# Recurrent outputs into dead input tiles, and a pair's decay sums into the chunks of the pair before

## The chip, the cores and the metric

The kernel runs on one core of one Trainium2 chip. The metric is device time in microseconds, the median of several runs. Engines: PE (matmuls), DVE (elementwise), ACT (activations and copies), POOL (elementwise, its own queue of transfers) and SP, which only issues transfers. Each runs its own list of instructions in order, and they wait for one another on semaphores.

## What is computed

One step of a decoder layer over 512 prompt tokens and 8 x 4 sample tokens (544 columns in all): three gated branches (sparse attention, RWKV-7 time mixing, cross-attention), then a squared-ReLU MLP. The change touches the second branch alone:

```python
def rwkv7_time_mix(p_b, shift_prev, wkv_prev, mu, ...):
    ps = p_b + (prev - p_b) * mu                      # prev: p_b one token earlier
    r, k, v, wl, al, gl = split_last(ps, RWKV_SIZES)
    w_log = -softplus(-(w0 + tanh(wl) @ w_up)) - 0.5
    decay = exp(-exp(w_log)); a = sigmoid(a0 + al @ a_up); g = sigmoid(gl) @ g_up
    kk = heads(k * k_k); kk = kk / max(sqrt(sum(kk * kk)), 1e-12)
    k_h = heads(k) * (1 + (a_h - 1) * k_a)
    # step: S = S*w_t + (S @ -kk_t)(kk_t*a_t)^T + v_t k_t^T ;  y_t = S @ r_t
    yn = (y - mean) * rsqrt(var + GN_EPS) * ln_g + ln_b   # group norm, per head
    bonus = sum(r_h * k_h * r_k) * v_h
    out = (yn + bonus) * g
```

## The kernel before

Everything lies with features on the 128 partitions and the 544 tokens along the columns. `pb3[:, t]` are the 14 projected tiles of the RWKV branch, each 553 columns wide: 0 to 3 hold r, 4 to 7 k, 8 to 11 v, for the four head pairs j (two heads of 64 features make one tile). `R` is a scratch area; its first slots of 544 columns are `r_`, `k__`, `v__`, `lw`, `L_`, `a_`, `kk`, `kh`, then `AR` (two), `bt`, `kt_`, `tA`, `tB`, each used by all four pairs in turn. `y_` is another name for `r_`.

A loop over j = 0 to 3 stands in every engine's list. For one pair the stages are, in PE's order:

- **prep**: DVE mixes r (`mix`, L2140 and L2143, from POOL's token difference `diff`, L814 to L818), sums the log-decays along the tokens (the scan L2228 into `L_`), takes off each chunk's middle (`c0`, L2234), notes the chunks' ends (`scf`, L2235 and L2236) and subtracts (L2237 into `a_`, signalled by `lx`). ACT then makes four exponentials (L1823 to L1826: `tA`, `tB`, `lw`, `scf`). DVE multiplies: L2243 (r, k and r_k into `L_`, signalled by `rk`), the factors `AR`, `bt`, `kt_`. PE sums `L_` over each head with the block matrix `blk` (the call `wide(6, ...)`, inside which the matmul is L1286), DVE makes the bonus of that into `L_` (L2250).
- **tm** and **inv**: PE transposes v, `bt`, `kt_` (L1328), and inverts a small triangular system by stages.
- **chunk** c = 0 to 3: 128 tokens each. PE computes z, u, the state's increment and y; ACT copies them out (y into `y_`); DVE updates the state `T0` (L2297, L2298). Beside it the next pair's work that needs no buffer of this pair is done, by calls of `early(j + 1, n)`: mixing k and v, `kk`, the decays and `a_`, the norm of `kk`.
- **dec**: the same recurrence for the sample tokens, with masks on DVE (from L2314 on) after products on PE (L1486 to L1488). PE first waits for the root of `kk` (ACT's L1789).
- **gn**: the group norm. PE sums `y_` by `blk`, DVE subtracts the mean (L2344), ACT squares and takes the root (L1910), DVE does `early(j + 1, 5)` and `(j + 1, 6)` (L2183; L2186 and L2187, which make `kh`), one or two weight conversions, the reciprocal (L2354) into `tB`, the product (L2355), `ln_g` and `ln_b` (L2359), the bonus (L2360) and the gate g (L2362), which goes into `pb3[:, j]` and signals `oB_out`.

Between these stages PE's list holds **fill** steps: pieces of other projections (the gates of the three branches), placed by `fill_plan` in fixed numbers per place (8 at each of three places in prep, 10 behind the transposes' wait, 2, 2 and 4 in a chunk, 4 in each part of dec, 6, 6 and 10 in gn). From the gates on a step is three matmuls (L980, L981, L982) on weights split in two parts: ACT copies the high part (`weights_hi`, L554), DVE makes the low part (`weights_lo`, L564, which I call a conversion). ACT evacuates a finished half of a gate by a tanh (L1653). In ACT's list the evacuations (`evacs`) stand at the places of the fills.

What sets the order at a turn from one pair to the next: POOL's `diff(r_, j)` waits for `oB_out`, since `r_` is `y_`; DVE's mix waits for that; the scan writes `L_`, which held the bonus until L2360.

## Time and profile before

| | |
|---|---|
| median of 3 runs | 1305.33 us (1304.65 to 1307.05) |
| the profiled execution: time, span | 1306.21 us, 1304.4 us |
| PE busy | 1218.8 us, 93% of the span |
| DVE, ACT, POOL busy | 707.3 us (54%), 407.4 us (31%), 88.1 us (7%) |
| mean granted clock of PE | 0.982 of full speed |
| transfers | 127.64 MB, 98 GB/s over the span |

A PE that is busy for 93% hides much of what the others do. The four pairs take the stretch from some 350 to 770 us. Timelines give the start and the length of each instruction and, in brackets, how long its engine was idle before it and what ended that. Lengths overlap a little: an engine's next instruction starts before the one before it is over. On PE three matmuls of a fill step start 0.126 us apart at full clock. The granted clock of a stretch is a share of full speed: 1.00 is 2.4 GHz, 0.50 is 1.2 GHz, and a value between means that it changed within the stretch.

### The profile page before, as it was taken

The page shows a single profiled execution, that of the slowest core. Times are in us where ns is not written, and L with a number is a line of the kernel's source. Part 1 is how long each engine was busy: PE and PEld are TensorE (multiplying, and loading weights), DVE is VectorE, ACT ScalarE, POOL GpSimd, SP SyncE. Part 2 cuts the span into 40 slices and gives each one's busy share as a digit, 9 for nine tenths or more (in the row PEclk, how much of TensorE's full clock was granted, in tenths as well). Part 3 has the DMA queues.
Part 4 walks back from the last instruction along what each step waited for, and adds up shares of the span by engine and source line. Part 5 has one row for each costly group of instructions (what it writes and reads, how often), then busy time and mean ns, then how long its engine had stood idle before and what let it go on. Part 6 is the DMA issues. An engine that isn't in the chain of part 4 may idle for free.

```text
span 1304.4 us, 25158 instructions
## 1 busy us (share of the span) xinstructions
PE 1218.8 (93%) x10594; PEld 1085.5 (83%) x10594; DVE 707.3 (54%) x1126; ACT 407.4 (31%) x792; POOL 88.1 (7%) x148
## 2 busy tenths in 40 slices
PE   7999987899999979989989999999999999999994
PEld 6658765577777778888878889999999999999994
DVE  6799998422431753473383267654535434444445
ACT  2111445334224332343333333233333133132120
POOL 1100000011020520002001020000000000000000
PEclk9999999999999989999999999999999999999997
DMA  9122535043100220131123125641222222222201
GB/s 333 41 102 85 200 118 182 33 162 130 77 11 34 82 91 11 60 107 51 52 93 109 37 86 169 210 169 65 98 86 109 74 88 98 92 71 97 97 33 69
DMA packets 39507, 127.64 MB, mean 98 GB/s; under 512 B 5235, under 2 KB 17523, under 8 KB 30179
## 3 DMA queue, kind: packets, MB, share of 16 engines
q1 hardware_dynamic: 36674, 120.95, 26.4%
q0 software_dynamic: 1440, 4.56, 1.0%
q8 instruction: 84, 1.38, 0.4%
q10 hardware_dynamic: 1280, 0.53, 0.2%
q14 instruction: 29, 0.23, 0.1%
HBM read 111.88 MB, written 14.13 MB: 97 GB/s over the span
## 4 chain that ended last, share of the span: by engine, by line
PE 75%; DVE 14%; SPq 4%; issue 3%; ACT 3%; DMA 1%; POOL 0%; DVEq 0%; ACTq 0%
PE ps L944 13%; PE ps L943 13%; PE ps L947 13%; PE ps L971 7%; PE ps L1335 4%; PE ps L980 4%; PE ps L981 3%; PE ps L982 3%; SPq L582 2%; SPq L581 2%; DVE R L2050 2%; PE ps L1286 2%; DVE small L2049 1%; PE ps L1072 1%; DVE R L2354 1%
## 5 line engine op out<-in xcount | busy, mean ns | idle before, releaser
L554 ACT ACTIVATE wh<-land 128x1024 fp32r<-128x1024 f32 (+1 forms) x120 | 116.2, 970 | 184.8 <-PE ps L947 184.8
L564 DVE TENSOR_TENSOR wl<-land,wh 128x1024 fp32r<-128x1024 f32 (+1 forms) x120 | 134.9, 1127 | 29.9 <-ACT wh L554 29.1
L971 PE MATMUL ps<-xn,ring 128*128 128x272 f32 x576 | 148.4, 400 | 0.0
L943 PE MATMUL ps<-xhi,wh 128*128 128x272 f32 x512 | 138.2, 288 | 2.3 <-DVE wl L564 1.2
L944 PE MATMUL ps<-hl,wh 128*128 128x272 f32 x512 | 138.2, 289 | 0.0
L944 PE MATMUL ps<-xlo,wh 128*128 128x272 f32 x512 | 138.1, 289 | 0.0
L943 PE MATMUL ps<-hh,wh 128*128 128x272 f32 x512 | 138.1, 288 | 0.0
L980 PE MATMUL ps<-xhi,wh 128*128 128x272 f32 x384 | 124.7, 325 | 2.3 <-issue 2.3
L971 PEld LDWEIGHTS ps<-xn,ring 128*128 128x128 f32 x576 | 104.1, 190 | 24.3 <-issue 6.2
L981 PE MATMUL ps<-xlo,wh 128*128 128x272 f32 x384 | 113.5, 295 | 0.0
L982 PE MATMUL ps<-xhi,wl 128*128 128x272 f32 x384 | 113.4, 295 | 0.0
L947 PE MATMUL ps<-hh,wl 128*128 128x272 f32 x512 | 106.1, 288 | 0.0
L947 PE MATMUL ps<-xhi,wl 128*128 128x272 f32 x512 | 106.1, 288 | 0.0
L943 PEld LDWEIGHTS ps<-xhi,wh 128*128 128x128 f32 x512 | 96.3, 188 | 2.9 <-DVE wl L564 1.7
L944 PEld LDWEIGHTS ps<-hl,wh 128*128 128x128 f32 x512 | 96.4, 188 | 0.0
L944 PEld LDWEIGHTS ps<-xlo,wh 128*128 128x128 f32 x512 | 96.4, 188 | 0.0
L943 PEld LDWEIGHTS ps<-hh,wh 128*128 128x128 f32 x512 | 96.3, 188 | 0.0
L980 PEld LDWEIGHTS ps<-xhi,wh 128*128 128x128 f32 x384 | 75.2, 196 | 13.0 <-issue 9.6
L947 PEld LDWEIGHTS ps<-xhi,wl 128*128 128x128 f32 x512 | 80.1, 188 | 0.0
L947 PEld LDWEIGHTS ps<-hh,wl 128*128 128x128 f32 x512 | 80.1, 188 | 0.0
L2398 DVE TENSOR_TENSOR mlpt<-mlpt 128x544 f32<-128x544 f32 x32 | 23.2, 724 | 104.8 <-ACT mlpt L1618 104.8
L2412 DVE TENSOR_TENSOR scaled<-ps,scaled 128x544 f32<-128x544 f32 x32 | 23.2, 725 | 102.4 <-PE ps L947 102.4
(413 smaller groups left out, 2351.3 us busy)
## 6 DMA issues: line engine op xcount, KB each, us to landing
land<-in_slabs SPq DMA_DIRECT2D x48, 1024.0 KB, 4.8
ring<-in_slabs SPq DMA_DIRECT2D x17, 1024.0 KB, 6.9
gates<-R SPq DMA_DIRECT2D x24, 272.0 KB, 2.0
merge<-gates SPq DMA_DIRECT2D x24, 272.0 KB, 4.2
land<-in_slabs SPq DMA_DIRECT2D x12, 512.0 KB, 3.9
xT<-in_mks SPq DMA_DIRECT2D x8, 512.0 KB, 5.7
R<-in_kv SPq DMA_DIRECT2D x24, 128.0 KB, 2.0
pb<-in_kv SPq DMA_DIRECT2D x24, 128.0 KB, 2.0
```

The lines of the kernel that those rows point to most:

```text
L554: act.activation(hi, src, ACT.Copy).then_inc(s["weights_hi"], 1)
L564: eng.tensor_tensor(lo, src, hi.bitcast(F32), ALU.subtract).then_inc(s["weights_lo"], 1)
L581: pg = eng.value_load(pages[0:1, 8 * b + j:8 * b + j + 1], min_val=0, max_val=i["ki"].shape[0] - 1)
L582: eng.dma_start(dst, pages_of[bass.ds(pg, 1)].rearrange("o p c -> (o p) c")).then_inc(sem, 16)
L943: pe.matmul(ps[:, b + h, 0:HALF], whi[:, k], hi[k][:, c], start=a, stop=False)
L944: pe.matmul(ps[:, b + h, 0:HALF], whi[:, k], lo[k][:, c], start=False, stop=False)
L947: mm = pe.matmul(ps[:, b + h, 0:HALF], wlo[:, k], hi[k][:, c], start=False, stop=z)
L971: mm = pe.matmul(ps[:, b, 0:HALF], W[:, k, c0_:c0_ + w], xn3[:, k, cols], start=a, stop=z)
L980: pe.matmul(ps[:, b, 0:HALF], whi[:, k], X[0][k][:, cols], start=a, stop=False)
L981: pe.matmul(ps[:, b, 0:HALF], whi[:, k], X[1][k][:, cols], start=False, stop=False)
L982: mm = pe.matmul(ps[:, b, 0:HALF], wlo[:, k], X[0][k][:, cols], start=False, stop=z)
L1335: mm = pe.matmul(out[q], left[q], right[q], start=True, stop=True)
```

## The change

Two buffers get separate homes for the time in which they collided. y of pair j goes into `pb3[:, j]`, the r input tile, which is dead once r is mixed; the bonus of pairs 0 to 2 into `pb3[:, 4 + j]`, the k input tile (pair 3 keeps `L_`). With that, `r_` and `L_` are free for the next pair while this one runs its chunks:

- POOL's `diff(r_, j + 1)` follows those of k and v, in pair j's inv stage, and no longer waits for `oB_out`.
- DVE does the next pair's scan and centring (`decay_sums`) in the third chunk, and the r mix, the ends and the subtraction (`decay_ends`, now into `lw`) and `early(j + 1, 6)` in the fourth.
- `bt` is made in gn, in the place where `early(j + 1, 6)` stood.
- ACT's exponentials wait for DVE's product y times `tB` (one count of `lx` more per pair) and stand ahead of the evacuations of prep's first place; that place's weight splits go with them.
- Of the two conversions that DVE had ahead of the exponentials' wait, the first stays ahead of it, the second follows the factors.

```diff
-        y_ = r_
+        def y_of(j):
+            return pb3[:, j, 0:TOK]
+        def bonus_of(j):
+            return pb3[:, 4 + j, 0:TOK] if j < 3 else L_
...
@@ POOL, for j in range(4)
-                if j:
-                    pool.wait_ge(s["oB_out"], j)
-                else:
+                if j == 0:
                     pool.wait_ge(s["t12"], 2)
-                diff(r_, j)
+                    diff(r_, 0)
...
                     diff(v__, 9 + j)
+                    diff(r_, j + 1)
...
@@ ACT, for j in range(4)
                     evacs("scan", 0)
-                else:
-                    evacs("prep", j, 0)
-                act.wait_ge(s["lx"], j + 1)
+                act.wait_ge(s["lx"], 2 * j + 1)
                 act.activation(tA, L_, ACT.Exp).then_inc(s["exps"], 1)
                 act.activation(tB, L_, ACT.Exp, scale=-1.0).then_inc(s["exps"], 1)
-                act.activation(lw, a_, ACT.Exp).then_inc(s["exps"], 1)
+                act.activation(lw, lw, ACT.Exp).then_inc(s["exps"], 1)
                 act.activation(scf, scf, ACT.Exp).then_inc(s["exps"], 1)
+                if j:
+                    evacs("prep", j, 0)
                 evacs("prep", j, 1)
...
@@ DVE
+            def decay_sums():
+                step(dve.tensor_tensor_scan(L_, k_("reset"), lw, 0.0, ALU.mult, ALU.add))
+                step(dve.tensor_copy(c0, L_[:, C // 2 - 1:SEQ:C]))
+                l3 = L_[:, 0:SEQ].rearrange("p (c t) -> p c t", c=4)
+                step(dve.tensor_tensor(l3, l3, c0.unsqueeze(2).to_broadcast([P, 4, C]), ALU.subtract))
+            def decay_ends():
+                step(dve.tensor_copy(scf, L_[:, C - 1:SEQ:C]))
+                step(dve.tensor_tensor(scf[:, 0:3], scf[:, 0:3], c0[:, 1:4], ALU.add))
+                dve.tensor_tensor(lw, L_, lw, ALU.subtract).then_inc(s["lx"], 1)
...
+                    mix(r_, 0, 4)
+                    decay_sums()
+                    dve.tensor_tensor(bt, kk, a_, ALU.mult)
+                    decay_ends()
                 else:
-                    dve.wait_ge(s["oB_out"], j)
-                mix(r_, j, 4 + 3 * j)
-                step(dve.tensor_tensor_scan(L_, k_("reset"), lw, 0.0, ALU.mult, ALU.add))
-                dve.tensor_tensor(bt, kk, a_, ALU.mult)
+                    weights_lo(dve, g + 2)
...
-                if j:
-                    weights_lo(dve, g + 2)
-                    weights_lo(dve, g + 3)
                 dve.wait_ge(s["exps"], 4 * (j + 1))
...
                 dve.tensor_tensor(kt_, kh, tB, ALU.mult).then_inc(s["factors"], 1)
+                if j:
+                    weights_lo(dve, g + 3)
                 dve.wait_ge(s["rk_sum"], j + 1)
-                dve.tensor_tensor(h2(L_), pair(6), h2(v__), ALU.mult).then_inc(s["bonus"], 1)
+                dve.tensor_tensor(h2(bonus_of(j)), pair(6), h2(v__), ALU.mult).then_inc(s["bonus"], 1)
...
                             early(j + 1, m)
+                        if c == 2:
+                            decay_sums()
+                        elif c == 3:
+                            mix(r_, j + 1, 4 + 3 * (j + 1))
+                            dve.wait_ge(s["state"], 4 * (j + 1))
+                            decay_ends()
+                            early(j + 1, 6)
...
                     early(j + 1, 5)
-                    early(j + 1, 6)
+                    dve.tensor_tensor(bt, kk, a_, ALU.mult)
...
                 step(dve.reciprocal(tB, tA))
-                step(dve.tensor_tensor(y_, y_, tB, ALU.mult))
+                if j < 3:
+                    dve.tensor_tensor(y_, y_, tB, ALU.mult).then_inc(s["lx"], 1)
+                    dve.wait_ge(s["lx"], 2 * j + 3)
+                else:
+                    step(dve.tensor_tensor(y_, y_, tB, ALU.mult))
...
-                step(dve.tensor_tensor(y_, y_, L_, ALU.add))
+                step(dve.tensor_tensor(y_, y_, bonus_of(j), ALU.add))
```

How instructions stand on an engine, before and after (line numbers differ between the two files). DVE at the end of pair 1's fourth chunk, from the state's update to the first sample mask, before:

```order
L2297 TENSOR_TENSOR small<-small,ps 128x64
L2298 TENSOR_SCALAR small<-small 128x64
L2314 TENSOR_TENSOR xT<-ps,cst 32x128
L2316 TENSOR_TENSOR xT<-ps,cst 32x32
L2318 TENSOR_TENSOR xT<-xT,cst 32x32
```

The same place after:

```order
L2308 TENSOR_TENSOR small<-small,ps 128x64
L2309 TENSOR_SCALAR small<-small 128x64
L2145 SCALAR_TENSOR_TENSOR R<-R,vec,pb 128x512
L2148 SCALAR_TENSOR_TENSOR R<-R,vec,pb 128x32
L2234 COPY small<-R 128x4
L2235 TENSOR_TENSOR small<-small 128x3
L2236 TENSOR_TENSOR R<-R 128x544
L2191 TENSOR_SCALAR R<-R,vec 128x544
L2192 SCALAR_TENSOR_TENSOR R<-R 128x544
L2332 TENSOR_TENSOR xT<-ps,cst 32x128
```

Seven operations, the r mix, the decays' ends and the two that make `kh`, now stand between the state's update and the masks.

DVE from the gate's product in pair 1 to L2243 in pair 2, before (the scan is printed as SCALAR_TENSOR_TENSOR with `cst`):

```order
L2362 TENSOR_TENSOR pb<-ps,R 128x544
L2140 SCALAR_TENSOR_TENSOR R<-R,vec,pb 128x512
L2143 SCALAR_TENSOR_TENSOR R<-R,vec,pb 128x32
L2228 SCALAR_TENSOR_TENSOR R<-cst,R 128x544
L2229 TENSOR_TENSOR R<-R 128x544
L2232 COPY small<-R 128x4
L2234 TENSOR_TENSOR R<-R,small 128x512
L2235 COPY small<-R 128x4
L2236 TENSOR_TENSOR small<-small 128x3
L2237 TENSOR_TENSOR R<-R 128x544
L564 TENSOR_TENSOR wl<-land,wh 128x1024 x2
L2243 SCALAR_TENSOR_TENSOR R<-R,vec 128x544
```

The same stretch after, from the group norm's reciprocal on:

```order
L2373 RECIPROCAL R<-R 128x544
L2375 TENSOR_TENSOR pb<-pb,R 128x544
L2382 TENSOR_SCALAR pb<-pb,vec 128x544
L2383 TENSOR_TENSOR pb<-pb 128x544
L2385 TENSOR_TENSOR pb<-ps,pb 128x544
L570 TENSOR_TENSOR wl<-land,wh 128x1024
L2252 SCALAR_TENSOR_TENSOR R<-R,vec 128x544
```

The nine operations from the mix to the subtraction and one of two conversions are gone from between the gate's product (L2362, now L2385) and L2243 (now L2252).

ACT at the turn from pair 0 to pair 1, from the group norm's root to the exponentials, before:

```order
L1910 ACTIVATE R<-ps,small 128x544
L1646 ACTIVATE pb<-ps 128x240
L1647 ACTIVATE pb<-ps 128x8x4
L1653 ACT_TABLE_LOAD
L1653 ACTIVATE R<-ps,small 128x272 x2
L554 ACTIVATE wh<-land 128x1024 x2
L1823 ACTIVATE R<-R 128x544
```

And after:

```order
L1915 ACTIVATE R<-ps,small 128x544
L1651 ACTIVATE pb<-ps 128x240
L1652 ACTIVATE pb<-ps 128x8x4
L1658 ACT_TABLE_LOAD
L1658 ACTIVATE R<-ps,small 128x272
L1826 ACTIVATE R<-R 128x544
L1827 ACTIVATE R<-R 128x544
L1828 ACTIVATE R<-R 128x544
L1829 ACTIVATE small<-small 128x4
L1658 ACTIVATE R<-ps,small 128x272
L560 ACTIVATE wh<-land 128x1024 x2
```

One gate evacuation and two weight splits have moved from ahead of the exponentials to behind them.

## Rows read from the trace of the kernel before

**Rows 1.** PE's waits: line, waited for, us in total, times, longest.

```profile
PE ps L1286 <- DVE R L2243: 13.0, 3, 5.0
```

**Rows 2.** Timeline of PE, turn from pair 0 to 1: start, length, instruction.

```profile
446.23 0.36 PE L980 MATMUL ps<-xhi,wh 128*128 128x272 f32 x1 [2.26 <-issue]
463.73 2.18 PE L1286 MATMUL ps<-R,cst 128*128 128x272 f32 x4 [5.02 <-DVE R L2243]
474.86 0.33 PE L1328 MATMUL ps<-cst,R 128*128 128x128 f32 x1 [0.58 <-ACT R L1653]
```

**Rows 3.** Timeline of PE, the other two turns.

```profile
574.13 1.18 PE L1286 MATMUL ps<-R,cst 128*128 128x272 f32 x4 [3.98 <-DVE R L2243]
...
584.19 0.33 PE L1328 MATMUL ps<-cst,R 128*128 128x128 f32 x1 [0.58 <-ACT R L1653]
...
681.94 0.82 PE L1286 MATMUL ps<-R,cst 128*128 128x272 f32 x1 [3.98 <-DVE R L2243]
...
693.18 0.33 PE L1328 MATMUL ps<-cst,R 128*128 128x128 f32 x1 [0.58 <-ACT R L1653]
```

**Rows 4.** Windows: length, busy us (count) of PE, PEld, DVE, ACT, POOL, clock, DMA.

```profile
449.11:458.16 9.05, 9.05 (x74) 9.05 (x73) 7.18 (x9) 2.87 (x4) 2.82 (x7) 1.00 0.45 170
463.73:469.10 5.37, 5.37 (x19) 4.91 (x20) 3.52 (x7) 1.43 (x2) 0.00 (x0) 0.50 0.62 229
537.00:541.00 4.00, 3.95 (x31) 3.69 (x32) 1.14 (x7) 1.49 (x2) 0.00 (x0) 0.58 0.02 4
```

**Rows 5.** Timeline of DVE, turn from pair 0 to 1.

```profile
441.04 1.26 DVE L2183 TENSOR_TENSOR R<-R 128x544 f32<-128x544 f32 x1
...
444.46 3.36 DVE L564 TENSOR_TENSOR wl<-land,wh 128x1024 fp32r<-128x1024 f32 x2
...
451.32 0.73 DVE L2355 TENSOR_TENSOR R<-R 128x544 f32<-128x544 f32 x1
...
460.62 2.35 DVE L564 TENSOR_TENSOR wl<-land,wh 128x1024 fp32r<-128x1024 f32 x2
462.89 0.78 DVE L2243 SCALAR_TENSOR_TENSOR R<-R,vec 128x544 f32<-128x544 f32 x1
```

**Rows 6.** Timeline of ACT, the same turn.

```profile
444.49 1.28 ACT L1653 ACT_TABLE_LOAD   x1
...
453.45 0.49 ACT L1653 ACTIVATE R<-ps,small 128x272 f32<-128x272 f32 x1 [2.51 <-PE ps L982]
453.84 2.00 ACT L554 ACTIVATE wh<-land 128x1024 fp32r<-128x1024 f32 x2
460.74 0.66 ACT L1823 ACTIVATE R<-R 128x544 f32<-128x544 f32 x1 [4.91 <-DVE R L2237]
```

**Rows 7.** Timeline of DVE, turn from pair 1 to 2.

```profile
554.96 0.72 DVE L2183 TENSOR_TENSOR R<-R 128x544 f32<-128x544 f32 x1
...
557.01 1.22 DVE L564 TENSOR_TENSOR wl<-land,wh 128x1024 fp32r<-128x1024 f32 x1
...
561.73 0.73 DVE L2355 TENSOR_TENSOR R<-R 128x544 f32<-128x544 f32 x1
...
566.27 0.75 DVE L2140 SCALAR_TENSOR_TENSOR R<-R,vec,pb 128x512 f32<-128x512 f32 x1 [1.69 <-POOL R L818]
...
567.10 1.28 DVE L2228 TENSOR_TENSOR_SCAN R<-cst,R 128x544 f32<-128x544 f32 x1
...
569.99 0.17 DVE L2235 COPY small<-R 128x4 f32<-128x4 f32 x1
...
571.03 2.35 DVE L564 TENSOR_TENSOR wl<-land,wh 128x1024 fp32r<-128x1024 f32 x2
```

**Rows 8.** Timeline of POOL in pair 0's group norm.

```profile
437.18 12.73 POOL L872 TENSOR_TENSOR xlo<-xn,xhi 128x272 fp32r<-128x272 f32 x12 [0.93 <-PE ps L971]
```

**Rows 9.** Timeline of DVE behind pair 1's last chunk.

```profile
537.53 0.28 DVE L2314 TENSOR_TENSOR xT<-ps,cst 32x128 f32<-32x128 f32 x1 [3.44 <-PE ps L1488]
```

**Rows 10.** Timeline of PE at the same place.

```profile
537.05 0.27 PE L1486 MATMUL ps<-R 64*32 64x64 f32 x2 [1.60 <-issue]
```

More of the change, by code:

```diff
@@ L1526, in _ @@
                 pe.wait_ge(s["s_y_out"], 2 * (j + 1))
-                wide(0, k_("blk"), y_).then_inc(s["mean"], 1)
+                wide(0, k_("blk"), y_of(j)).then_inc(s["mean"], 1)
                 fill("gn", j, 0)
@@ L1873, in _ @@
                     act.wait_ge(s["ychunk"], n + 1)
-                    act.activation(y_[:, C * c:C * (c + 1)], ps[:, 6, 0:P], ACT.Copy).then_inc(s["y_chunk"], 1)
+                    act.activation(y_of(j)[:, C * c:C * (c + 1)], ps[:, 6, 0:P], ACT.Copy).then_inc(s["y_chunk"], 1)
                     if j < 3:
@@ L1902, in _ @@
                     act.wait_ge(s["s_y"], n + 1)
-                    act.activation(y_[hp, SEQ:TOK], ps[hp, 4 + hh, 256:256 + NS], ACT.Copy).then_inc(s["s_y_out"], 1)
+                    act.activation(y_of(j)[hp, SEQ:TOK], ps[hp, 4 + hh, 256:256 + NS], ACT.Copy).then_inc(s["s_y_out"], 1)
                 evacs("dec", j, 3)
@@ L1906, in _ @@
                 act.wait_ge(s["yc"], j + 1)
-                act.activation(tA, y_, ACT.Square).then_inc(s["yc_sq"], 1)
+                act.activation(tA, y_of(j), ACT.Square).then_inc(s["yc_sq"], 1)
                 evacs("gn", j, 0)
@@ L2224, in _ @@
                         early(0, n)
-                else:
-                    dve.wait_ge(s["oB_out"], j)
-                mix(r_, j, 4 + 3 * j)
-                step(dve.tensor_tensor_scan(L_, k_("reset"), lw, 0.0, ALU.mult, ALU.add))
-                dve.tensor_tensor(bt, kk, a_, ALU.mult)
+                    mix(r_, 0, 4)
+                    decay_sums()
+                    dve.tensor_tensor(bt, kk, a_, ALU.mult)
+                    decay_ends()
+                else:
+                    weights_lo(dve, g + 2)
                 dve.wait_ge(s["mix"], 2 + 3 * (j + 1))
-                step(dve.tensor_copy(c0, L_[:, C // 2 - 1:SEQ:C]))
-                l3 = L_[:, 0:SEQ].rearrange("p (c t) -> p c t", c=4)
-                step(dve.tensor_tensor(l3, l3, c0.unsqueeze(2).to_broadcast([P, 4, C]), ALU.subtract))
-                step(dve.tensor_copy(scf, L_[:, C - 1:SEQ:C]))
-                step(dve.tensor_tensor(scf[:, 0:3], scf[:, 0:3], c0[:, 1:4], ALU.add))
-                dve.tensor_tensor(a_, L_, lw, ALU.subtract).then_inc(s["lx"], 1)
-                if j:
-                    weights_lo(dve, g + 2)
-                    weights_lo(dve, g + 3)
                 dve.wait_ge(s["exps"], 4 * (j + 1))
@@ L2343, in _ @@
                 dve.wait_ge(s["mean"], j + 1)
+                y_ = y_of(j)
                 dve.scalar_tensor_tensor(h2(y_), pair(0), -1.0 / 64, h2(y_), ALU.mult, ALU.add).then_inc(s["yc"], 1)
```

## The prediction

> **What bounds the kernel now.** I read the page first: PE is busy for 93% of the span (the table above), so time can only go where PE waits or runs slowly. PE's list of waits is the second view. The longest wait in the part that the change touches is L1286, the `blk` product that sums the bonus, on DVE's L2243: 13.0 us in 3 times, the longest 5.0 [rows 1]. There is one at each turn from a head pair to the next. Third, PE's timeline at the turn from pair 0 to pair 1 [rows 2]: PE has used up the fill steps that it may do, comes to the product at 458.71 (463.73 less 5.02) and starts it at 463.73. The other two turns wait 3.98 us each [rows 3]. The clock shows that the wait costs more than its length: in the 5.37 us after it the granted clock is 0.50, the lower of the two levels (1.2 GHz), PE having stood still just before [rows 4].
>
> Then the timelines of DVE and ACT at that turn tell what ends last [rows 5, 6]. DVE finishes the group norm, waits for POOL's token difference, mixes r, scans, centres and only then frees ACT's exponentials (460.74); two weight conversions later comes L2243 at 462.89. At the turn from 1 to 2 the same stretch, mix to the end of the last subtraction, runs from 566.27 to 571.03 [rows 7], behind a group-norm product (L2355) that was over at 562.46. From there to L2243 lies nothing that needs the group norm's result, only its buffers: y and r share one, the bonus and the scan share another. That is what the change undoes.
>
> **Part 1, the wait.** After the change the exponentials need tA and tB free, that is the end of L2355, and nothing else that is late. Turn 0 to 1: L2355 ends at 452.05 now; part 3 brings that to 451.2. The exponentials take at most 2.15 us (460.74 to the reader at 462.89): 453.35. ACT now evacuates a gate half and splits weights behind them (0.49 and, for the first of two, 1.0) [rows 6]: 454.8. DVE, whose last three group-norm operations end by 453.3, waits for that, converts (half of 2.35: 1.18) and does L2243 (0.78): 456.8. PE comes at 458.71 less 0.9, 457.8. Margin 1.0 us, the wait is gone. Turn 1 to 2: 562.46 plus 2.15 for the exponentials and as much for DVE's three operations beside them (they end at 564.58, 566.27 less 1.69 [rows 7]), one conversion, L2243: 566.6, where PE comes at 574.13 less 3.98, 570.15. Margin 3.6 us; turn 2 to 3 repeats it. I take all 13.0 us. What is late next: PE itself. The transposes (L1328) want bonus and factors, and 18 fill steps, 6.8 us, lie between; the conversion put in front of the bonus fits there.
>
> **Part 2, the clock after the wait.** A fill step, three matmuls, takes 0.377 us at full clock: 74 matmuls, two of them cut by the edges, so 24 steps, in 9.05 us [rows 4]. From the product to the transposes there are the product (1.18 at the turn from 1 to 2 [rows 3], the next matmul starting inside it; I take 0.9), 18 steps (6.8), the tail of the last matmul (taken as 0.16) and the wait for its evacuation (0.58): 8.44 us. It took 11.13, 10.06 and 11.24 [rows 2, 3]. Excess 2.7 + 1.6 + 2.8 = 7.1 us. With no standstill ahead of it I count all of it as gained. Bounds: 0, if the clock falls anyway, and 7.1.
>
> **Part 3, a shorter queue before pair 0's first weights.** PE also stands 2.26 us at 446.23 until DVE has converted the first gate weights, a conversion that starts at 444.46 behind two operations for the next pair (L2186, L2187) after 442.30 [rows 2, 5]. The change takes these two (2.16 us) out and puts one product (`bt`) in. L2183 beside POOL's conversions took 1.26 there [rows 5] and 0.72 alone [rows 7], so `bt` costs 0.76 to 1.3 and the gain is 0.9 to 1.4. I take 0.9, since POOL is busy to 449.9 [rows 8]. The Trainium skill, "SBUF — State Buffer", says under its rules on contention that the port pair of DVE and GpSimd is an exclusive lock, so that the loser blocks for the other's whole instruction. By that `bt` could wait for a full POOL piece (12.73 over 12, 1.06 us) and the gain would be 0.4, half a microsecond less in the sum; the 0.54 us that L2183 lost is half such a piece.
>
> **Part 4, what the chunks take on.** About 5.4 us of DVE work per pair move into pairs 0 to 2: into the third chunk the scan, copy and centring (567.10 to 571.03 without `bt` and the last 1.04: about 2.25 us), into the last chunk the mix (0.83), the ends of the decay (1.04) and the two kh operations (1.3, from 557.01 less 554.96, less L2183): 3.2 us [rows 7]. PE needs DVE next when the state is updated and, after the last chunk, for the sample masks (L2314). In pair 1 DVE has nothing to do for 3.44 us ahead of 537.53, when PE's products reach it [rows 9], so 3.2 us just fit; PE itself stands 1.60 us there, until 537.05, for a square root on ACT that does not move [rows 10]. Behind the masks PE still has four fill steps, 1.5 us. I cost it at nothing; without that cover it is at most 3 x 5.4. The weight conversion behind the third chunk comes 2.2 us later, and its weights are wanted a chunk and more later. POOL does one token difference more before the state's DMA, 1.7 us by DVE's wait on one at 566.27, with most of a pair to spare. SP's queue keeps its order. ACT stores y into another tile with the same shape. The odd pitch of the new tiles is free for the reads that show it (L2140 reads such a tile), and where DVE writes there it has the margins above.
>
> **Sum.** 13.0 + 7.1 + 0.9 = 21.0 us. The profiled execution has a span of 1304.4 and a time of 1306.21; 1283.4 and 1285.2 would follow. Against the median of the runs, 1305.33, it is **1284.3**.
>
> **Rivals.** *The turn from 0 to 1 keeps a wait.* Its margin is only 1.0 us and hangs on ACT's evacuation and split in one row. If ACT is 2.6 us later than I count, 1.6 us of wait stay and with them that turn's 2.7 us of slow clock: 1284.3 + 4.3 = 1288.6. For it: conversions beside POOL take longer, 3.36 for two against 2.35 [rows 5]. Against: POOL ends before them.
>
> *A short wait at every turn, and the clock falls all the same.* The 1.60 us standstill in pair 1 is followed by 0.58 of the clock [rows 4, 10], so a short wait can be enough. Three waits of 1.6 and the whole 7.1 kept: 1284.3 + 11.9 = 1296.2. Against: 3.6 us of margin at two turns.
> A path to it: the exponentials now follow the norm's square root on ACT. A table load took 1.28 us at 444.49, ahead of a gate's tanh [rows 6]; one ahead of the exponentials would use up the first margin and leave 2.3 at the others, a wait of 0.3 at one turn. I see none there now, and the tanh still comes between: 1 in 50, inside this rival.
> The Trainium skill, "ScalarE: Activation LUTs", section on table sets, charges 2.66 us for every switch between the sets of root and exponential, which would make that wait 1.7 us; it puts tanh and exp in one set, as the trace does with no load at L1823.
>
> *The chunks pay.* The moved DVE operations run late into the sample masks, all 5.4 us of them on PE's path, and each new standstill costs a slow stretch like the first turn's: 3 x (5.4 + 2.7) = 24.3, less 21.0: **1308.6, slower**. It begins to cost when the last chunk's share exceeds 3.44 us, and turns the sign only if PE's own fill steps cover none of it. Operations 1.75 times as long, as beside POOL, would do the first; POOL is idle in that chunk.
>
> *Nothing moves.* The weights' supply paces the fill steps, so PE waits for conversions instead: about 1305. Against: PE's waits on conversions are at pair 0's start and behind the pairs only.
>
> **How the numbers follow.** Forecast 0.72, first turn late 0.11, short wait at every turn 0.08, nothing moves 0.04, chunks pay 0.05. Within the forecast the slow stretch of pair 1 (12 matmuls at half pace, about 1.3 us) may vanish or another may come, and part 3 has 0.5 either way: 1281.5 to 1287. With the first rival and half the way to the second the range is 1280.5 to 1292, which leaves out under 2 in 10. A measurement of this kernel tells 0.2%, 2.6 us, from no change. Faster by more: 0.91; within: 0.04; slower: 0.05.
>
> **What would show it.** Right: PE has no wait on the `blk` product of the bonus, granted clock 1.00 from there to the transposes, about 8.4 us between them; the exponentials start within 0.2 us of the end of the y product; the first gate's wait is near 1.4 us; the pairs' chunks keep their length. Wrong: a wait of PE for the masks behind the last chunk, an idle ACT before the exponentials that ends with DVE long after the group norm, or the clock at 0.50 in the old places without a wait ahead of it.

## The result, and the profile after

The changed kernel takes **1283.22 us** (median of 6 runs, 1281.55 to 1284.41) against 1304.7 for the kernel before beside it: a ratio of 0.983, 95% interval 0.982 to 0.984, **faster by 21.5 us**. The forecast was 1284.3 with a range of 1280.5 to 1292. Run again later, beside the experiments e7, e8 and e9, it took 1283.61 (1282.02 to 1284.83); that is the base for all of them below. A few executions (three of the kernel before, two each of e1 and e4, one each of e3 and e5) were 1 to 2% longer than the rest at a lower mean granted clock; the medians are over all runs, and leaving these out moves none by more than 0.7 us. The profiled execution took 1281.81 us with a span of 1280.0, 24.4 us less than the profiled one of before.

In the changed file the lines have moved: the `blk` product is L1291 (was L1286), the transposes L1333, the product of r L2252 (was L2243), the group norm's product L2375, the first exponential L1826, a weight conversion L570.

PE's list of waits no longer has the bonus product. PE's timeline at the turn from pair 0 to 1 and at the next turn, which answer to [rows 2, 3] (start, length, instruction, idle before):

```profile
445.12 0.36 PE L985 MATMUL ps<-xhi,wh 128*128 128x272 f32 x1 [1.33 <-ACT pb L1652]
...
457.44 1.08 PE L1291 MATMUL ps<-R,cst 128*128 128x272 f32 x4
...
465.88 0.66 PE L1333 MATMUL ps<-cst,R 128*128 128x128 f32 x4 [0.58 <-ACT R L1658]
...
559.49 1.08 PE L1291 MATMUL ps<-R,cst 128*128 128x272 f32 x4
...
567.94 0.66 PE L1333 MATMUL ps<-cst,R 128*128 128x128 f32 x4 [0.58 <-ACT R L1658]
```

The rows of the two products show no idle time ahead of them, and product to transposes takes 8.44 and 8.45 us (forecast 8.44). The windows between them at the three turns (length, busy time of PE, PEld, DVE, ACT and POOL with counts, granted clock, DMA) answer to the second line of [rows 4]:

```profile
457.44:465.88 8.44, 7.87 (x60) 7.49 (x58) 4.28 (x6) 2.46 (x5) 0.00 (x0) 1.00 0.49 159
559.49:567.94 8.45, 7.88 (x60) 7.50 (x58) 1.95 (x2) 2.46 (x5) 0.00 (x0) 1.00 0.46 157
661.53:669.98 8.45, 7.87 (x61) 7.50 (x59) 1.95 (x2) 2.46 (x5) 0.00 (x0) 1.00 0.46 159
```

The granted clock is 1.00 in all three, where it was 0.50 just behind the first wait. DVE and ACT at the first turn, DVE first, which answer to [rows 5, 6]:

```profile
442.15 1.17 DVE L2366 TENSOR_TENSOR R<-R 128x544 f32<-128x544 f32 x1
443.24 3.48 DVE L570 TENSOR_TENSOR wl<-land,wh 128x1024 fp32r<-128x1024 f32 x2
...
450.22 0.72 DVE L2375 TENSOR_TENSOR pb<-pb,R 128x544 f32<-128x544 f32 x1
...
454.18 1.23 DVE L570 TENSOR_TENSOR wl<-land,wh 128x1024 fp32r<-128x1024 f32 x1 [1.12 <-ACT wh L560]
455.32 0.78 DVE L2252 SCALAR_TENSOR_TENSOR R<-R,vec 128x544 f32<-128x544 f32 x1
...
459.77 0.72 DVE L2261 TENSOR_TENSOR pb<-ps,R 128x544 f32<-128x544 f32 x1
```

```profile
444.31 1.28 ACT L1658 ACT_TABLE_LOAD   x1
...
450.98 0.66 ACT L1826 ACTIVATE R<-R 128x544 f32<-128x544 f32 x1 [1.15 <-DVE pb L2375]
```

The exponentials start 0.04 us after the group norm's product ends (450.94), where they waited 4.91 us for the scan's last subtraction. The product of r ends at 456.1, PE comes at 457.44: a margin of 1.3 us, forecast 1.0. At the next turn L2252 ends at 555.7 and PE comes at 559.49: 3.8, forecast 3.6. No table load stands ahead of L1826; the one for the tanh came at 444.31, as before.

Behind pair 1's last chunk, DVE and then PE, which answer to [rows 9, 10]:

```profile
528.62 0.28 DVE L2332 TENSOR_TENSOR xT<-ps,cst 32x128 f32<-32x128 f32 x1 [0.48 <-PE ps L1493]
```

```profile
528.07 0.27 PE L1491 MATMUL ps<-R 64*32 64x64 f32 x2 [1.60 <-issue]
```

DVE's 3.44 us of idle time ahead of the sample masks have become 0.48: the moved work just fits, as forecast.

**Where the 24.4 us of the two profiled executions went.** 13.0 is the wait. Product to transposes took 11.13, 10.06 and 11.24 and takes 8.44, 8.45 and 8.45: 7.1. The first gate's wait went from 2.26 to 1.33: 0.9. That is 21.0, the forecast's sum. 0.5 more lies in how the waits are counted: the gap starts where the last matmul ends (458.71 at the first turn), 0.16 us after the next could have started (458.55), at each of three turns. The other 2.9 show when the starts of the same PE instruction are set side by side.

1.5 is a stretch of slow clock in pair 1's sample part which the changed kernel's execution does not have, though PE stands 1.60 us ahead of it in both: the changed kernel leads by 8.98 us at the sample products (537.05 against 528.07) and by 10.47 a few products on (541.22 against 530.75). In windows of the kernel before:

```profile
536.00:538.00 2.00, 0.95 (x14) 0.94 (x15) 0.43 (x3) 1.97 (x3) 0.00 (x0) 0.91 0.01 1
538.00:540.00 2.00, 2.00 (x11) 2.00 (x11) 0.60 (x4) 0.14 (x1) 0.00 (x0) 0.50 0.04 8
540.00:542.00 2.00, 2.00 (x39) 1.66 (x40) 0.29 (x2) 0.49 (x1) 0.00 (x0) 0.74 0.00 0
```

Length times one less the clock is 0.18 + 1.0 + 0.52, 1.7 us, an estimate that takes PE as the bound there. A second such stretch of the kernel before alone, behind the pairs, is worth nothing, although its first window looks the same. It follows a wait of 2.33 us for weights that both executions have (at 779.27 and 756.07). The changed kernel, which runs on at full clock, then waits once more for weights, and the kernel before does not. Window and waits of the kernel before, then of the changed one:

```profile
780.00:782.00 2.00, 2.00 (x12) 2.00 (x11) 1.97 (x4) 0.80 (x2) 0.00 (x0) 0.50 0.26 102
PE ps L943 <- DVE wl L564: 3.6, 2, 2.3
```

```profile
PE ps L948 <- DVE wl L570: 5.0, 3, 2.3
...
763.96 0.36 PE L948 MATMUL ps<-bhi,wh 128*128 128x272 f32 x1 [1.42 <-DVE wl L570]
```

The lead is 23.2 us ahead of the stretch and 23.2 again at that instruction (787.15 against 763.96). Of the rest, 1.0 lies in the last stretch of the kernel, from PE's last products to the end (14.77 us from 1289.63, 13.77 from 1266.23): the clock is at 0.50 there in both, but in the changed kernel's execution it fell only after these products. 0.4 lies in small pieces elsewhere. Other executions have such stretches in other places (below), so the medians differ by 21.5 and not by 24.4.

### The profile page after: what moved, and what is told of

Read it like the earlier page. It is cut to its first block, busy times and chain, and to the rows that moved or that the text cites. A ratio compares the mean times of both kernels' runs of the same rounds, so it can differ in the third digit from the quotient of the medians.

```text
span 1280.0 us, 25157 instructions
## 1 busy us (share of the span) xinstructions
PE 1206.3 (94%) x10594; PEld 1075.2 (84%) x10594; DVE 707.1 (55%) x1126; ACT 407.8 (32%) x792; POOL 87.8 (7%) x148
## 3 DMA queue, kind: packets, MB, share of 16 engines
q8 instruction: 84, 1.38, 0.4%
## 4 chain that ended last, share of the span: by engine, by line
PE 80%; DVE 10%; SPq 4%; ACT 3%; issue 3%; DMA 1%; DVEq 0%; ACTq 0%
PE ps L949 13%; PE ps L948 13%; PE ps L952 13%; PE ps L976 8%; PE ps L985 5%; PE ps L1340 4%; PE ps L987 4%; PE ps L986 4%; SPq L588 2%; PE ps L1291 2%; SPq L587 2%; DVE R L2055 2%; DVE small L2054 1%; PE ps L1077 1%; DVE small L2120 1%
## 5 line engine op out<-in xcount | busy, mean ns | idle before, releaser
L570 DVE TENSOR_TENSOR wl<-land,wh 128x1024 fp32r<-128x1024 f32 (+1 forms) x120 | 135.3, 1128 | 26.7 <-ACT wh L560 25.9
L948 PE MATMUL ps<-xhi,wh 128*128 128x272 f32 x512 | 138.2, 288 | 2.3 <-DVE wl L570 1.2
L949 PE MATMUL ps<-xlo,wh 128*128 128x272 f32 x512 | 138.1, 289 | 0.0
L985 PE MATMUL ps<-xhi,wh 128*128 128x272 f32 x384 | 121.3, 316 | 1.3 <-ACT pb L1652 1.3
L987 PE MATMUL ps<-xhi,wl 128*128 128x272 f32 x384 | 110.8, 289 | 0.0
L986 PE MATMUL ps<-xlo,wh 128*128 128x272 f32 x384 | 110.6, 288 | 0.0
L952 PE MATMUL ps<-xhi,wl 128*128 128x272 f32 x512 | 106.1, 288 | 0.0
L948 PEld LDWEIGHTS ps<-xhi,wh 128*128 128x128 f32 x512 | 96.3, 188 | 2.9 <-DVE wl L570 1.7
L985 PEld LDWEIGHTS ps<-xhi,wh 128*128 128x128 f32 x384 | 72.2, 188 | 11.9 <-issue 7.0
L2421 DVE TENSOR_TENSOR mlpt<-mlpt 128x544 f32<-128x544 f32 x32 | 23.2, 724 | 104.8 <-ACT mlpt L1623 104.8
L2435 DVE TENSOR_TENSOR scaled<-ps,scaled 128x544 f32<-128x544 f32 x32 | 23.2, 725 | 102.4 <-PE ps L952 102.4
```

Source lines behind the costliest of these rows:

```text
L570: eng.tensor_tensor(lo, src, hi.bitcast(F32), ALU.subtract).then_inc(s["weights_lo"], 1)
L948: pe.matmul(ps[:, b + h, 0:HALF], whi[:, k], hi[k][:, c], start=a, stop=False)
L949: pe.matmul(ps[:, b + h, 0:HALF], whi[:, k], lo[k][:, c], start=False, stop=False)
L952: mm = pe.matmul(ps[:, b + h, 0:HALF], wlo[:, k], hi[k][:, c], start=False, stop=z)
L985: pe.matmul(ps[:, b, 0:HALF], whi[:, k], X[0][k][:, cols], start=a, stop=False)
L986: pe.matmul(ps[:, b, 0:HALF], whi[:, k], X[1][k][:, cols], start=False, stop=False)
```

## The experiments

All times are medians, set against 1283.6 for the changed kernel and 1306.1 to 1306.6 for the one before, which ran beside each group of them. Lines shift a little in the experiments' files: in the rows below L2254 is the product of r, L2146 the mix of r, L2261 or L2263 the bonus, L2336 or L2337 the last operation of the sample masks, and L1495 or L1497 the product that reads it.

### Is the slow clock the standstill's doing?

**e1_pe_busy**: the kernel before, with PE given something to do while it waits.

```diff
+                for n in range((0, 11, 8, 8)[j]):
+                    pe.matmul(ps[:, n % 2, 0:HALF], k_("blk"), t13[:, 0:HALF], start=True, stop=True)
                 pe.wait_ge(s["rk"], j + 1)
                 wide(6, k_("blk"), L_).then_inc(s["rk_sum"], 1)
```

> The kernel before, with products whose results nobody reads put on PE just ahead of its wait for the bonus product: 11 of 128x272 at the turn from pair 0 to 1 and 8 at each of the other two, about 0.46 us each (two took 0.92 us at full clock), so 5.1 and 3.7 us where PE stood 5.0, 4.0 and 4.0. DVE is as late as before. Theory (the slow stretch follows PE's standstill): the wait ends when it did, but the granted clock stays at 1.00 behind it, product to transposes is about 8.4 us at each turn, and 7 us of the time go: about 1297.6 us. Rival A (the clock falls there anyway, by what the chip does at that time): no gain, 1304 to 1305, the clock at 0.50 in the same places. Rival B (only the first turn's wait is long enough): 2.7 us, 1302.

It took 1299.68 us, 6.6 less than the kernel before. Ten of its twelve runs lie between 1298.9 and 1301.3, below all 28 of the kernel before (1304.6 to 1308.7); over all twelve the 95% interval of the ratio is 0.994 to 1.000. The windows from the product to the transposes:

```profile
466.26:474.70 8.44, 7.86 (x59) 7.49 (x57) 3.07 (x4) 2.46 (x5) 0.00 (x0) 1.00 0.32 131
572.48:581.03 8.55, 7.98 (x58) 7.60 (x58) 4.42 (x7) 2.46 (x5) 0.00 (x0) 1.00 0.45 157
678.79:687.33 8.54, 7.97 (x58) 7.59 (x58) 4.42 (x7) 2.46 (x5) 0.00 (x0) 1.00 0.44 155
```

DVE is as late as before (10.83 us from the end of the group norm's product to the product of r, 10.84 in the kernel before) and the clock holds at 1.00. The theory holds, and rivals A and B fall: part 2's 7.1 us are a cost of PE's standing still, and they can be had even without removing the wait. The time is 2 us above the theory's 1297.6, and 1.5 of that is the edit's own doing: at the first turn the added products ran on past the product of r, which had ended at 464.76.

```profile
461.21 5.21 PE L1316 MATMUL ps<-pb,cst 128*128 128x272 f32 x22
466.26 1.08 PE L1286 MATMUL ps<-R,cst 128*128 128x272 f32 x4
```

**e5_dve_late_7us** and **e4_dve_late_3us** go the other way: the changed kernel with DVE made late again, by two reciprocals or by one (the edit of e5; e4 has a 1 for the 2).

```diff
+                for _ in range(2 if j else 0):
+                    step(dve.reciprocal(L_, tA))
                 dve.scalar_tensor_tensor(L_, r_, v_("rwkv_r_k", j), kh, ALU.mult, ALU.mult).then_inc(s["rk"], 1)
```

> The changed kernel with two reciprocals of 3.54 us, whose results are overwritten, on DVE just ahead of the product that PE's bonus sum waits for, in pairs 1 to 3. Theory: PE waits there again, 5.8 us at the first turn (margin 1.3 less 7.1) and 3.3 at the other two (margin 3.8), 12.4 in all, and the clock falls behind each wait as it did in the kernel before, 2.7 + 1.6 + 2.8 us: 1283.2 + 19.5 = 1302.7. Rival (the clock was not the wait's doing): 1283.2 + 12.4 = 1295.6, granted clock 1.00 behind the waits.

It took 1302.16 us (1298.8 in the profiled execution). PE's waits and the three windows behind them, in that execution:

```profile
PE ps L1291 <- DVE R L2254: 12.3, 3, 5.7
```

```profile
464.21:474.31 10.10, 9.53 (x58) 8.84 (x58) 5.56 (x8) 2.46 (x5) 0.00 (x0) 0.84 0.41 133
571.37:580.42 9.05, 8.20 (x58) 7.64 (x59) 5.46 (x8) 2.46 (x5) 0.00 (x0) 1.00 0.47 146
677.48:686.53 9.05, 8.20 (x59) 7.64 (x59) 5.46 (x8) 2.47 (x5) 0.00 (x0) 1.00 0.42 146
```

The waits are those expected, 12.3 against 12.4. The median is the theory's 1302.7, but its profile is not: the clock fell at the first wait only (5.74 us), not at the two of 3.29, and 10.10 + 9.05 + 9.05 is 2.9 us over three times 8.44. So 1283.6 + 12.3 + 2.9 = 1298.8 explains the profiled execution, which is the fastest of the eleven. The mean granted clock of every execution is on record: it is 0.988 or 0.989 in the five that took up to 1300.8 us and 0.984 to 0.986 in the five from 1302.2 to 1305.0. So the longer ones had more slow clock; at which waits, no profile shows.

> The changed kernel with one reciprocal of 3.54 us ahead of the product that PE's bonus sum waits for, in pairs 1 to 3. Theory (the margins are 1.3 us at the first turn and 3.8 at the others): PE waits 2.2 us at the first turn and not at the others; 1283.6 + 2.2 = 1285.8, with up to 2.7 more if the clock falls behind the wait. Rival (the margins are smaller than the trace reads): waits at all three turns, 1290 or more.

It took 1288.09. PE waits for the product of r once, 2.1 us, at the first turn, as the margins say; the clock stayed at 1.00 behind it:

```profile
PE ps L1291 <- DVE R L2254: 2.1, 1, 2.1
...
PE ps L985 <- DVE pb L2263: 0.5, 2, 0.3
...
PE ps L985 <- DVE R L2263: 0.2, 1, 0.2
```

The last two rows are new and were in no sum. They show where the 0.6 us in each of e5's windows of 9.05 at full clock comes from: the ninth fill step behind the bonus product waits for the bonus itself. Here product to transposes is 9.06 at the first turn and 8.92 at the other two, where PE did not wait for the product at all. With 2.15 + 0.6 + 0.5 + 0.5 = 3.75 the time would be 1287.4.

### Which part of the change carries the gain?

**e2_y_in_r**: the group norm's tile goes back to r's.

```diff
         def y_of(j):
-            return pb3[:, j, 0:TOK]
+            return r_
...
-                if j == 0:
+                if j:
+                    pool.wait_ge(s["oB_out"], j)
+                else:
                     pool.wait_ge(s["t12"], 2)
-                    diff(r_, 0)
+                diff(r_, j)
...
-                    diff(r_, j + 1)
...
                 else:
                     weights_lo(dve, g + 2)
+                    mix(r_, j, 4 + 3 * j)
...
-                            mix(r_, j + 1, 4 + 3 * (j + 1))
```

> The changed kernel with y back in r's tile, so that POOL's difference and the mix of r wait for the end of the group norm again; the bonus, the scan, the ends of the decay and the kh operations stay moved. Theory (the exponentials need only the scan, r only the bonus product behind them): group norm ends at about 453.3 at the first turn, POOL's difference 1.7, mix 0.83, product of r 0.78 bring 456.9 where PE comes at 457.4: margin 0.5, no wait, and 2.3 us less work in DVE's last chunk is worth nothing: 1283 to 1284 us, same as the changed kernel. Rival (both tiles must be split): the wait on DVE is back at the first turn, 1 to 2 us, with its slow clock 2.7: 1287 to 1288.

It took 1285.75 (four runs, 1285.18 to 1289.43; ratio to before 0.984 to 0.987), some 2 us over the changed kernel. No wait on the product of r came back. DVE at the first turn:

```profile
455.78 0.75 DVE L2146 SCALAR_TENSOR_TENSOR R<-R,vec,pb 128x512 f32<-128x512 f32 x1
...
456.73 0.78 DVE L2254 SCALAR_TENSOR_TENSOR R<-R,vec 128x544 f32<-128x544 f32 x1
```

The product of r ends at 457.5 and PE comes at 457.57: of the expected margin of 0.5, 0.1 is left. The bonus behind it is late, and the first turn's product to transposes takes 9.05. PE is 0.75 us behind the changed kernel from the second turn on. The rest of the 2 us is not the turns': up to 889.09 in its profiled execution nothing is added to the 0.75, and behind that PE loses 1.6 us more, spread evenly over 380 us (889.09 to 1268.60, against 888.36 to 1266.23 in the changed kernel) which the edit does not touch. y's move is worth 0.75 us by the trace, the first turn's, and some 2 at most by the medians.

**e3_bonus_in_L**: the bonus goes back to the scan's tile, so that the scan, the centring and the ends of the decay must follow the group norm's last sum.

```diff
         def bonus_of(j):
-            return pb3[:, 4 + j, 0:TOK] if j < 3 else L_
+            return L_
...
                 else:
+                    decay_sums()
+                    decay_ends()
                     weights_lo(dve, g + 2)
...
-                        if c == 2:
-                            decay_sums()
-                        elif c == 3:
+                        if c == 3:
                             mix(r_, j + 1, 4 + 3 * (j + 1))
-                            dve.wait_ge(s["state"], 4 * (j + 1))
-                            decay_ends()
                             early(j + 1, 6)
...
```

> The changed kernel with the bonus back in the scan's tile: scan, centring and ends of the decay (3.3 us on DVE) run behind the group norm's last sum again, at the start of the pair; y stays out of r, and the mix and the kh operations stay in the chunks. Theory: exponentials start 3.3 us after the group norm's end, 456.3 at the first turn, product of r ready at 459.2, PE comes at 457.4: a wait of about 1.8 us at the first turn, none at the others (559.1 against 559.5, margin 0.4). With the first turn's slow stretch of 2.7 us: 1283.2 + 4.5 = 1287.7; if the clock does not fall after a wait this short, 1285. Rival (this split carries nothing, y's does all): 1283. Rival (it carries nearly all): 1295 or more.

It took 1296.68: 13.1 lost where the theory had 4.5 at most. The number is that of the last rival, and its reason (the bonus's split carries nearly all of the gain) is not what the trace shows. PE's waits name another place than I had watched:

```profile
PE ps L985 <- ACT R L1658: 7.5, 3, 3.3
```

The fill steps themselves wait, for ACT's evacuation of a gate half. ACT at the first turn:

```profile
457.61 0.66 ACT L1826 ACTIVATE R<-R 128x544 f32<-128x544 f32 x1 [6.56 <-DVE R L2236]
...
459.36 0.47 ACT L1658 ACTIVATE R<-ps,small 128x272 f32<-128x272 f32 x1
```

The changed kernel put the exponentials ahead of that evacuation. Late exponentials, on an engine that works in order, hold it up, and PE's next fill step with it. **e12_bonus_in_L_gate_first** is the same kernel with ACT's old order, to tell this from the lateness itself:

```diff
+                else:
+                    evacs("prep", j, 0)
                 act.wait_ge(s["lx"], j + 1)
...
                 act.activation(scf, scf, ACT.Exp).then_inc(s["exps"], 1)
-                if j:
-                    evacs("prep", j, 0)
...
```

> The kernel with the bonus back in the scan's tile (which took 1296.7), but with ACT's gate evacuation ahead of the exponentials, as in the kernel before. Theory (what that kernel lost was the gate evacuation queued behind late exponentials on ACT, for which PE's fill steps waited 3.3, 2.1 and 2.1 us, not the product of r): no wait of PE on ACT at the gate's steps; the product of r late by 1.8 us at the first turn and 0.4 at the others: 1283.6 + 2.6 = 1286.2, up to 1289 with a slow stretch. Rival (DVE's 3.3 us behind the group norm are the loss wherever ACT's evacuation stands): 1295 to 1297.

1288.42: 8.3 us come back, and the gate's wait on ACT is gone.

```profile
PE ps L1291 <- DVE R L2254: 2.3, 3, 1.6
...
PE ps L985 <- DVE R L2263: 0.8, 3, 0.3
```

2.3 us for the product of r (expected 2.6), and 0.6 at each turn for the late bonus, 1.8: 1287.7. So the bonus's move is worth 4.4 us with the old order on ACT (against e11, which follows) and 13.1 with the new one.

**e11_gate_before_exp** is the changed kernel with ACT's old order alone (the edit just shown).

> The changed kernel with ACT's first gate evacuation of the pair and its weight splits ahead of the exponentials again, as in the kernel before; all DVE and tile changes stay. Theory: at the first turn the evacuation can start at about 452.4, two splits end at 454.8, the exponentials at 457.0 and the product of r at 457.7, where PE comes at 457.4: a wait of 0.3 and none at the others: 1284 to 1285. Rival (the order on ACT is what made the margin everywhere): waits of 1 to 2 us at each turn, 1288 or more. Rival (it is worth nothing): 1283.6.

1284.04 (1283.87 to 1286.51), within the spread of the changed kernel. The new order on ACT gains 0.4 us by the medians, less than the runs spread, and is the part that punishes a late scan. Together: 4.4 us for one tile and 0.75 to 2 for the other do not add up to 22. By the rows above, either split alone already takes enough of DVE's work from behind the group norm to bring DVE about level with PE, and what comes on top is margin. The change's third part on DVE, the second conversion moved behind the factors, was not undone by itself: by its row it is 1.22 us (458.64), nearly the whole margin of the first turn.

### What do the chunks still hide?

**e6_chunk_late_3us**: one more reciprocal in the last chunk.

```diff
                             dve.wait_ge(s["state"], 4 * (j + 1))
+                            step(dve.reciprocal(tB, lw))
                             decay_ends()
```

> The changed kernel with a reciprocal of 3.54 us, whose result is overwritten, on DVE ahead of the decay's ends in the last chunk of pairs 0 to 2. Theory (the moved work fits by 0.48 us of idle DVE and by what is left of PE's fill steps, about 0.6 us, in pair 1; by the latter alone in pair 0): PE waits for the sample masks 2.5 us in pairs 1 and 2 and 3.1 in pair 0: 8.1 us, 1291.7, more if the clock falls behind these waits (2.7 each at most, 1300). Rival (PE has cover elsewhere in the sample part): under 3 us, 1286.

1297.08, in between the two figures of the theory. PE's waits, and the first of them in its timeline with the clock behind it:

```profile
PE ps L1497 <- DVE xT L2337: 7.5, 6, 2.6
```

```profile
427.06 0.24 PE L1497 MATMUL ps<-xT 32*32 32x32 f32 x2 [2.62 <-DVE xT L2337]
427.57 0.24 PE L1497 MATMUL ps<-xT 32*32 32x32 f32 x2 [0.27 <-DVE xT L2337]
```

```profile
427.06:432.50 5.44, 5.17 (x49) 4.19 (x50) 2.19 (x9) 0.32 (x2) 0.00 (x0) 0.56 0.01 3
538.36:544.40 6.04, 5.77 (x63) 5.07 (x64) 3.47 (x11) 0.64 (x4) 0.00 (x0) 0.72 0.00 0
```

7.5 us of the added 10.7 (three times 3.58, the reciprocal with the gap behind it) reach PE, 8.1 expected. In pair 0 it is 2.62 + 0.27 of 3.58, so 0.7 us of cover was left there, and 1.3 in the others. The other 6 us of the time are, to some 0.2, slow clock: 0.44 of 5.44 and 0.28 of 6.04 in these windows are 2.4 and 1.7, and pair 2 has a third such stretch. What doesn't fit in the chunks costs its length and some 0.8 of it again. The rival in which the chunks pay had 2.7 us of slow clock for each such wait; here it is 2.4, 1.7 and 1.7.

**e8_late_root_wait** takes away PE's 1.60 us behind the chunks, by waiting for the square root only where its banks are written.

```diff
-                if j < 3:
-                    pe.wait_ge(s["kk_rt"], j + 2)
                 pe.wait_ge(s["t0s_in"], 16 * (j + 1))
...
+                if j < 3:
+                    pe.wait_ge(s["kk_rt"], j + 2)
                 for hh, n, hp, d in heads:
                     pe.matmul(ps[0:NS, hh, 0:64], d["m4"][0:NS, 2], tms[0:NS, 0, hp], start=True, stop=False)
```

> The changed kernel with PE's wait for the next pair's square root (1.60, 1.60 and 0.44 us ahead of the sample products) moved behind the four fill steps, to the products that write the banks which the root is read from. PE then reaches the sample products at 526.47 in pair 1 in place of 528.07. Theory (the moved operations fill DVE to 528.15, so DVE is next): the masks come 0.47 us earlier, not 1.6, and PE waits for them behind its fill steps: gain 0.5 to 1.0 at each of two turns, none at pair 0: 1281.3 to 1282.2. Rival (DVE's chunk work has cover to spare): 1.6 + 1.6 + 0.4 gained, 1279.6. Rival (a new short wait and a slow stretch): 1283 to 1286.

1281.02 (1279.7 to 1282.08), 2.6 us less, between theory and first rival. In pair 1 PE's sample products start as soon as its fill steps end, and the masks hold it up by a little:

```profile
525.80 0.30 PE L1489 MATMUL ps<-R 64*32 64x64 f32 x2
...
528.74 0.24 PE L1495 MATMUL ps<-xT 32*32 32x32 f32 x2 [0.27 <-DVE xT L2336]
```

**e7_weights_first** converts pair 0's first weights ahead of the two operations for the next pair (moved, not changed), and **e9_root_kh_weights** joins this to e8 and moves the two kh operations out of the last chunk, to behind the block products:

```diff
                             decay_ends()
-                            early(j + 1, 6)
...
+                if j < 3:
+                    early(j + 1, 6)
                 if j:
                     weights_lo(dve, g + 8)
```

> The changed kernel with pair 0's first two gate weights converted ahead of the two operations for the next pair, so that the conversions can start at about 440.9 in place of 443.24. Theory (DVE's conversion ends PE's wait of 1.33 us at the first gate step): the wait falls to what ACT's last evacuation of the stage before leaves, which ends at 444.29 against PE's start at 445.12: 0.8 us gained; with the conversions beside POOL's pieces at 1.74 each, 0.8 at least is hidden. 1282.4 us. Rival (PE waits for ACT's evacuation alone, as the wait's row names it): 0. Rival (the two operations come late for what follows, the reciprocal at 446.65): slower by up to 0.5.

1282.75 (1281.72 to 1284.93): 0.9 less, which the spread of runs does not settle. In its profile the wait of 1.33 us is gone altogether: PE starts the first gate step at 443.94, ahead of the end of ACT's evacuation L1652 (444.80).

```profile
443.94 0.49 PE L985 MATMUL ps<-xhi,wh 128*128 128x272 f32 x1
...
444.60 0.20 ACT L1652 ACTIVATE pb<-ps 128x32 f32<-128x32 f32 x1
```

So PE had waited for DVE's conversion there, though the row names ACT, and my bound of 0.8 rested on the wrong engine. PE then comes to the first turn earlier and waits for the bonus (`L985 <- DVE pb L2261: 0.3`), which takes some 0.5 back.

> The changed kernel with the edits of the two kernels ahead of it and the two kh operations (1.2 us) moved from the last chunk to behind the block products of the sample part, where DVE is idle. Theory: DVE is through with the chunk's work at 526.9, as PE's sample products come, so the whole of PE's 1.6 us goes at both turns: 3.2 + 0.4 + 0.8 from the first weights = 4.4 less: 1278.8. Rival (the chain of the sample part, DVE and ACT, is late by as much as PE comes earlier): 1282.

**1279.24** (1278.18 to 1280.02), 4.4 us less than the changed kernel as expected, and no run of the one reaches a run of the other. It is the best of all. PE's waits no longer have L1491, nor the masks; of the places of this study it keeps these:

```profile
PE ps L1333 <- ACT R L1658: 1.7, 3, 0.6
...
PE ps L1333 <- DVE pb L2261: 1.4, 1, 1.4
...
PE ps L985 <- DVE pb L2261: 0.3, 1, 0.3
```

## Why the prediction was right, step by step

| step | forecast | measured |
| --- | --- | --- |
| 1, wait for the bonus product | -13.0 us; margins 1.0 and 3.6 | gone; 1.3 and 3.8; e4 waits 2.1 at the first turn alone |
| 2, product to transposes | -7.1, to 8.44 us each | 8.44, 8.45, 8.45; e1 alone: -6.6 |
| 3, first gate's wait | -0.9, to 1.4 | 2.26 to 1.33 |
| 4, chunks | 0, DVE's 3.44 us just filled | 0.48 left, no wait; e6 measures 0.7 to 1.3 of cover |
| sum | 21.0 | 21.5 by the medians |

**The number.** The sum of 21.0 is what the parts measure in the two profiled executions, besides the 0.5 in the counting of the gaps. That the medians differ by 21.5 is luck to within a few microseconds: slow stretches came and went in places that the change does not touch, and made 24.4 of it in the profiled pair. The prediction had allowed for that in its range (the stretch of pair 1 may vanish or another may come), not in its sum.

**Part 1** held for the reason given: nothing between the group norm and the product of r needed the norm's result. What it underrated is its own dependence on ACT. It counted the gate's evacuation as work behind the exponentials, which it is, but not that PE's fill steps wait for that evacuation; e3 shows that this order costs 8 us as soon as the scan is late. In the changed kernel it is not late, so nothing came of it.

**Part 2** was right in size and cause. One sentence in part 1 was wrong in detail: that 18 fill steps lie between the product and the wait for the bonus. Eight lie there (3.0 us, then the wait, then ten more), as e4's row with L2263 shows. The bonus ends at 460.49 at the first turn and PE's ninth step starts at 461.38, so 0.9 us is left there, where I had counted on ten steps, 3.8 us, more.

**Part 3.** `bt` beside POOL's pieces took 1.17 us (442.15) where it takes 0.73 alone at the next turn (545.23), 0.44 more; the gain was 0.93. The Trainium skill, "SBUF — State Buffer", has under "Who interferes with whom" that a DVE instruction with two SBUF inputs and a GpSimd instruction that reads SBUF lock one another out for a whole instruction. The prediction made a gain of 0.4 of that, an estimate with `bt` held for a POOL piece of 1.06. The trace agrees that they hold one another up, and speaks against 1.06 for a piece: that was a mean over pieces which DVE held up too. Four pieces in a row, with DVE idle or in a reciprocal, take 0.75 each, and the two beside `bt` and the operation ahead of it 1.24 each (441.50 and 442.70). So `bt` lost a little over half of an unhindered piece. The four, which overlap a little:

```profile
433.17 2.91 POOL L877 TENSOR_TENSOR xlo<-xn,xhi 128x272 fp32r<-128x272 f32 x4 [12.25 <-PE ps L976]
```

**Part 4** was right with little to spare, and the row that said so was DVE's 3.44 us. The chunks kept their length: from the transposes to pair 1's sample products PE takes 62.19 us in both kernels (474.86 to 537.05, 465.88 to 528.07). POOL's and the weights' part showed nothing: the one new wait of PE for weights (1.42 us at 763.96) is in e1 too, which has the order of the kernel before, and in every other profiled execution without a slow stretch ahead of it.

**The rivals.** The first turn kept no wait; e2, with 1.2 us less margin, had 0.1 left. The table load ahead of the exponentials did not come: behind the load for the gate's tanh (444.31) no other stands ahead of L1826. The Trainium skill, "ScalarE: Activation LUTs", puts tanh and exp in one set under "Table sets", and the trace agrees. The same page of the Trainium skill, under "What ACT_TABLE_LOAD costs", counts 2.66 us for a switch, 1.28 of it for the load and 1.38 for a drain. The trace agrees with the load, 1.28 in its rows, and shows no drain: at the next turn the load for the root starts at 545.28, 0.02 us behind the activation before it, and the root follows 0.14 behind the load. The chunks did not pay; e6 shows what they cost when they do.

## What to carry to other kernels

Where the bounding engine waits once per pass for a chain on another engine, look in that chain for steps that need only a buffer of the stage before; a dead tile for the result can free them, and only the steps that bring the late engine ahead of the bounding one count. Before moving something ahead of an evacuation on an in-order engine, ask who waits for the evacuation when the moved step is late. A standstill of TensorE costs its length and, in part of the executions, a slow stretch as well (7.1 us on 13.0 here, some 6 on 7.5 in e6), so giving it any work, or a wait placed a few steps later, is worth trying by itself. And before a slow stretch is counted as a loss, look at PE's next wait: behind the pairs it took the whole of it back.

## What the hardware showed that I had not expected

The granted clock after a standstill is not settled by the standstill's length. PE stands 1.60 us in pairs 1 and 2 in eleven of the profiled executions (both kernels, the changed one a second time, and e1 to e5, e7, e11 and e12), 22 times; a stretch at 0.50 followed in 4 of them: in the kernel before in pair 1, and in pair 2 in e3, e7 and the second profile of the changed kernel, whose first had none there. Waits of 5.02 and 5.74 us came with one, and both of 3.98; those of 3.29 in e5 did not, nor one of 3.32 in e3, while one of 2.62 in e6 did. PE's wait for the first gate weights, 2.3 us, had none behind it in the kernel before and had one in e1; the wait of 2.33 for weights behind the pairs, which all have, had one in the kernel before, e3, e9 and e11 and none in the ten other profiled executions. Those ten wait 1.4 us for the next weights 7.9 us later, and the four do not. A prediction that counts on the clock has to leave 2 or 3 us for it either way.
